# Two fused transformer blocks on one core: the first modulation and the stages' entries in another order, and identity products on TensorE at its waits

## The chip, the cores and the metric

One of the eight cores of a Trainium2 chip runs the whole program in one launch. The metric is the device time of one execution in microseconds. The engines are named as the profile names them: PE (TensorE matmul), PEld (its weight loads), DVE (VectorE), ACT (ScalarE), POOL (GpSimd), SP (SyncE, which issues nearly all DMAs).

## The reference

A block of two layers (feed-forward, mixer, feed-forward; the first mixer is differential attention over 512 image and 256 context tokens, the second a Fourier mixer), then a block with sparse and banded attention and a mixture of experts, all in float32 with 1024 channels. What the change touches:

```python
def rms_norm(x, g):
    y = x32 * lax.rsqrt(jnp.mean(x32 * x32, axis=-1, keepdims=True) + EPS)
    return (y * g.astype(jnp.float32)).astype(x.dtype)

def swiglu(h, w_gu, w_d):
    g, u = jnp.split(h @ w_gu, 2, axis=-1)
    return (jax.nn.silu(g) * u) @ w_d

def ada_params(cond, w_mod, b_mod):
    m = jax.nn.silu(cond) @ w_mod + b_mod          # 9 vectors of 1024 per layer: shifts, scales, gates

for i in range(DEPTH):
    x = x + 0.5 * mx[2] * swiglu(modulate(rms_norm(x, norm_g[i, 0]), mx[0], mx[1]), ...)
    ...   # mixer with mx[3..5], second feed-forward with mx[6..8]; the same for the context y in layer 0
```

## The kernel before

The program is a row of stages, each a `Block` in which every engine has its own hand-written list of instructions, ordered by semaphores. At a block's end every engine drains its queue and all meet, so the next stage starts when the last of them is through. Channels lie on the partitions (8 tiles of 128) and tokens on the free axis. A float32 product of full precision is written as three products of a high and a low part (`three`: wh·xh, wh·xl, wl·xh), with ACT making the high part of weights and inputs and DVE (or POOL) the low part.

`start` loads x (`xy`) and computes the modulation vectors that the first feed-forward needs: 17 tiles of 128 outputs, in five parts (`parts`, four of 512 columns and a last one of 128). Each part is a product of the condition with a slab `w[c]` in four column groups of PE (L443), copied by ACT (`line`, L488), turned to columns by `turn` (L435), and added to its bias by DVE. Meanwhile ACT squares x tile by tile (`square_tile`, L254) and DVE sums the squares (`add_square`, L259).

The entry of most stages is a norm: PE sums the squares over channels (`sum_squares`, L269 and L272), ACT takes the root (`token_roots`, L286), DVE inverts it (`invert_roots`, L291), PE spreads the roots over the partitions with products against the identity (`spread_roots`, L279), and then, tile by tile, DVE scales x (L859), ACT adds the shift and makes the high part (L789), DVE the low part (L865), and PE takes the tile (L711 to L713). The weights of the first two slabs were prefetched; ACT and POOL split them meanwhile (`early_high`, `early_low`).

`feed_forward` runs phases of gate/up and down products over slabs of a ring with two slots (`ring`, s = 0 and 1). Per slab SP loads (L656), ACT makes the high part (`split`, L755), DVE the low part (`split`, L805), PE multiplies (L675 to L677), and ACT and DVE finish the result (`item`). `split_ahead` gives ACT and DVE the order: the split of the next slab stands before the item of this one. In two of the four feed-forwards DVE also computes the later modulation vectors (`sum_mod_turn`, L368), whose weights SP loads (`load_mod_turn`, L354); `mod=0` in the first, over 768 tokens (image and context), `mod=1` in the second. `gains_of_mods` turns them to gains before the last down phase. The four are, in order: ffn1 of layer 0 (768 tokens), ffn2 of layer 0, ffn1 of layer 1 and ffn2 of layer 1 (512 tokens each).

`first_mixer` has an entry of its own: `w_high(i)` (L1104) makes the high parts of six heads' weights, four of them from the prefetched slabs and the last two (Y and Z) from a slab that SP loads in the stage, and `in_high` (L1138) the high part of the input; PE starts with the first three heads (L1013 to L1015) side by side.

## Time and profile before

| | |
|---|---|
| three executions | 3363.56, 3373.28 and 3377.71 us, median 3373.28 us |
| the profiled execution | 3363.18 us by the same clock; its span in the trace is 3360.3 us |
| PE, PEld, DVE, ACT, POOL busy | 91%, 67%, 41%, 25%, 7% of the span |
[...]

[...] A plain float32 product of the program is two records in the trace, one that is declared as fp32r is one. A matmul's duration has a tail that overlaps the next one: steady steps are shorter than the durations.

### The profile page before, as it was taken

What the parts mean: (1) busy time and instruction counts of PE and PEld (TensorE: products, weight loads), DVE (VectorE), ACT (ScalarE), POOL (GpSimd) and SP (SyncE); (2) the same over time, 40 slices, a digit from 0 to 9 for tenths busy, and PEclk for the clock granted to TensorE, in tenths of its full rate; (3) what the DMA queues carried; (4) which work ended last, traced back from release to release, by engine and by line L of the source; (5) the groups of instructions that cost most, each with busy time, mean ns of one, the idle gap of its engine ahead of it and who ended that gap; (6) DMA issues with size and microseconds to landing.
All of it is one profiled execution on the core that took longest, in us unless ns stands there. A gap on an engine that the chain in (4) does not pass through costs nothing. (4 is left out here: it accounts for less than half of the span.)

```text
span 3360.3 us, 36972 instructions
## 1 busy us (share of the span) xinstructions
PE 3073.8 (91%) x14470; PEld 2264.8 (67%) x14470; DVE 1375.7 (41%) x2137; ACT 847.1 (25%) x1334; POOL 241.7 (7%) x273
## 2 busy tenths in 40 slices
PE   6999999799888899999999899999999689869996
PEld 4888888677644687877888546888788454343334
DVE  3646454535565463644333213333421284121112
ACT  3211111232354332223222202222323252011111
POOL 1000000001000100001000001000100151012220
PEclk8999999899998899999999999999999799979997
DMA  4423323211000354632232202232222200338883
GB/s 185 159 93 120 118 98 128 79 62 51 13 0 26 140 224 156 238 138 88 94 106 77 80 25 88 88 100 91 86 98 81 91 2 28 139 141 348 351 347 127
DMA packets 78198, 395.15 MB, mean 118 GB/s; under 512 B 17536, under 2 KB 19968, under 8 KB 51712
## 3 DMA queue, kind: packets, MB, share of 16 engines
q1 hardware_dynamic: 66560, 385.12, 31.0%
q0 software_dynamic: 11520, 8.43, 0.8%
q8 instruction: 78, 1.28, 0.2%
q14 instruction: 40, 0.33, 0.0%
HBM read 443.82 MB, written 16.78 MB: 137 GB/s over the span
## 5 line engine op out<-in xcount | busy, mean ns | idle before, releaser
L675 PE MATMUL ps<-h_high_ffn,weights_high_ffn 128*128 128x512 f32 (+1 forms) x1696 | 624.7, 368 | 13.6 <-DVE weights_low_ffn L805 8.8
L676 PE MATMUL ps<-h_low_ffn,weights_high_ffn 128*128 128x512 f32 (+1 forms) x1696 | 623.6, 368 | 0.0
L677 PE MATMUL ps<-h_high_ffn,weights_low_ffn 128*128 128x512 f32 (+1 forms) x1696 | 623.0, 367 | 0.0
L675 PEld LDWEIGHTS ps<-h_high_ffn,weights_high_ffn 128*128 128x128 f32 x1696 | 320.1, 189 | 69.6 <-issue 14.2
L677 PEld LDWEIGHTS ps<-h_high_ffn,weights_low_ffn 128*128 128x128 f32 x1696 | 320.1, 189 | 53.0
L676 PEld LDWEIGHTS ps<-h_low_ffn,weights_high_ffn 128*128 128x128 f32 x1696 | 320.2, 189 | 52.5
L675 PE MATMUL ps<-hidden_high_ffn,weights_high_ffn 128*128 128x512 f32 (+1 forms) x880 | 328.5, 373 | 17.1 <-DVE weights_low_ffn L805 9.7
L755 ACT ACTIVATE weights_high_ffn<-weights 128x2048 fp32r<-128x2048 f32 (+4 forms) x160 | 243.9, 1524 | 364.8 <-PE ps L677 275.6
L676 PE MATMUL ps<-hidden_low_ffn,weights_high_ffn 128*128 128x512 f32 (+1 forms) x880 | 327.0, 372 | 0.0
L677 PE MATMUL ps<-hidden_high_ffn,weights_low_ffn 128*128 128x512 f32 (+1 forms) x880 | 326.9, 372 | 0.0
L805 DVE TENSOR_TENSOR weights_low_ffn<-weights,weights_high_ffn 128x2048 fp32r<-128x2048 f32 (+4 forms) x160 | 289.7, 1811 | 88.7 <-ACT weights_high_ffn L755 87.1
L814 DVE TENSOR_TENSOR tmp<-ps,tmp 128x512 f32<-128x512 f32 x110 | 68.1, 636 | 430.0 <-ACT tmp L765 430.0
L765 ACT ACTIVATE tmp<-ps 128x512 f32<-128x512 f32 x110 | 58.6, 554 | 645.0 <-PE ps L677 641.3
L675 PEld LDWEIGHTS ps<-hidden_high_ffn,weights_high_ffn 128*128 128x128 f32 x880 | 167.8, 191 | 48.6 <-issue 10.1
L676 PEld LDWEIGHTS ps<-hidden_low_ffn,weights_high_ffn 128*128 128x128 f32 x880 | 167.9, 191 | 28.1
L677 PEld LDWEIGHTS ps<-hidden_high_ffn,weights_low_ffn 128*128 128x128 f32 x880 | 167.5, 190 | 28.6
L829 DVE SCALAR_TENSOR_TENSOR xy<-ps,mods,xy 128x512 f32 (+1 forms) x112 | 72.6, 672 | 262.2 <-PE ps L677 261.8
L2623 PE MATMUL ps<-big,work 128*64 128x512 f32 x768 | 171.6, 598 | 5.1 <-issue 4.1
L368 DVE CUSTOM_DVE_ANT_0 scratch_ffn<-scratch_ffn 128x1024 f32<-128x1024 f32 x127 | 151.4, 1220 | 1.6 <-DMA scratch_ffn<-in_w_mod 1.6
L2623 PEld LDWEIGHTS ps<-big,work 128*64 128x64 f32 x768 | 65.8, 138 | 107.0 <-issue 107.0
L254 ACT ACTIVATE tmp<-xy 128x512 f32<-128x512 f32 (+3 forms) x64 | 43.7, 684 | 364.4 <-DVE xy L829 150.8
L315 POOL TENSOR_TENSOR weights_low_ffn<-weights,weights_high_ffn 128x512 fp32r<-128x512 f32 x32 | 40.8, 1288 | 1214.6 <-ACT weights_high_ffn L306 1214.6
(399 smaller groups left out, 4303.4 us busy)
## 6 DMA issues: line engine op xcount, KB each, us to landing
weights<-in_ffn_gu SPq DMA_DIRECT2D x88, 1024.0 KB, 5.0
big<-in_w_exp_gu SPq DMA_DIRECT2D x32, 2048.0 KB, 9.6
scratch_ffn<-in_w_mod SPq DMA_DIRECT2D x35, 1536.0 KB, 6.4
weights<-in_ffn_d SPq DMA_DIRECT2D x24, 768.0 KB, 4.3
weights<-in_w_in SPq DMA_DIRECT2D x16, 1024.0 KB, 4.8
weights<-in_ffn_d SPq DMA_DIRECT2D x24, 640.0 KB, 3.9
weights<-in_w_exp_dn SPq DMA_DIRECT2D x15, 1024.0 KB
hbuf<-in_w_exp_dn SPq DMA_DIRECT2D x12, 1024.0 KB
```

The costliest lines, as they stand in the source:

```text
L254: scalar.activation(last_square[:, 0:cols], x, ACT.Square).then_inc(nm["squared"].sem, 1)
L315: gpsimd.tensor_tensor(quarter(w_low[:, s, :], c), quarter(ring.buf[:, s, :], c), quarter(w_high[:, s, :], c).bitcast(F32), ALU.subtract). ...
L368: vector.tensor_tensor_reduce(mod_w[b][:, j, :] if last else mod_product, mod_w[b][:, j, :], cond_row[:, c, :], 1.0, 0.0, ALU.mult, ALU.ad ...
L675: pe.matmul(out, wh, xh, start=(k == 0), stop=False)
L676: pe.matmul(out, wh, xl, start=False, stop=False)
L677: mm = pe.matmul(out, wl, xh, start=False, stop=(k == n - 1))
L755: scalar.activation(w_high[:, s, 0:n], ring.buf[:, s, 0:n], ACT.Copy).then_inc(high_done[s].sem, 1)
L765: scalar.activation(tmp[:, s, a:a + n], gate_up(s, 0, c), ACT.Silu).then_inc(silu_g[s].sem, 1)
L805: vector.tensor_tensor(w_low[:, s, 0:n], ring.buf[:, s, 0:n], w_high[:, s, 0:n].bitcast(F32), ALU.subtract).then_inc(ring.used[s], 1)
L814: vector.tensor_tensor(tmp[:, s, a:a + n], gate_up(s, 1, c), tmp[:, s, a:a + n], ALU.mult)\
L829: vector.scalar_tensor_tensor(x, down(s, c), g, x, ALU.mult, ALU.add)\
L2623: mm = pe.matmul(ps[b * CAP:(b + 1) * CAP, 2 + n % 2, :], gT[:, k, b * CAP:(b + 1) * CAP], w[:, k, :], start=(k == 0), stop=(k == KD - 1))
```

## The change

Five edits. (1) `start`: the 128-wide part comes first, two parts are in flight on SP, the norm of the first feed-forward (sum of squares, roots, spread) is moved into `start` between the products, and the first feed-forward is called with `rooted=True` and leaves it out. (2) `feed_forward`: SP reloads slot 0 ahead of the modulation's loads, and slot 1 behind the first ones. (3) `split_ahead` has a `pause`: the gains (and, for `mod=0`, the last `sum_mod_turn`) are done by DVE after the second item of the last down phase. (4) `first_mixer`: ACT's `w_high(3)` to `w_high(5)` stand between the `in_high`. (5) `keep_busy(pe, n)`: n products of the identity with itself into an unused PSUM bank; three ahead of each spread (nine places), and nine at nine places: after the spread in three feed-forwards and both mixers, at the end of three feed-forwards, and at the end of the first mixer's output projection.

```diff
+    def sum_squares(pe, cols, ahead=0):
+        pe.wait_ge(nm["summed"].sem, nm["summed"].at + ahead)
...
+    def keep_busy(pe, n):
+        for _ in range(n):
+            pe.matmul(ps[:, 4, 0:P], ident[:], ident[:], start=True, stop=True)
+
     def spread_roots(pe, cols):
+        keep_busy(pe, 3)
         pe.wait_ge(nm["rooted"].sem, nm["rooted"].at + 2)
...
     def start(nxt):
-        parts = [4 * P] * (MOD_BEFORE[0] // 4) + [MOD_BEFORE[0] % 4 * P]
+        parts = [MOD_BEFORE[0] % 4 * P] + [4 * P] * (MOD_BEFORE[0] // 4)
...
                 for c, n in enumerate(parts):
-                    if c > 0:
-                        sync.wait_ge(tables.sem, 16 * c)
-                        sync.dma_start(w[c][:], io["w_mod_first"][c, :, :, 0:n]).then_inc(tables.sem, 16)
+                    if c >= 2:
+                        sync.wait_ge(mod_landed[c % 2].sem, 16 * (c // 2))
+                    sync.dma_start(w[c][:], io["w_mod_first"][c, :, :, 0:n]).then_inc(mod_landed[c % 2].sem, 16)
...
+                product(0)
+                product(1)
+                pe.wait_ge(tables.sem, 32)
+                turn(0)
+                turn(1)
+                pe.wait_ge(const_set.sem, 2)
+                sum_squares(pe, NT, KD)
+                product(2)
+                spread_roots(pe, NT)
+                turn(2)
+                product(3)
+                turn(3)
+                product(4)
+                turn(4)
...
                 for c in range(len(parts)):
+                    if c == 2:
+                        token_roots(scalar, NT)
                     scalar.wait_ge(sm["product"].sem, c + 1)
                     scalar.activation(line[c][:], ps[:, c, 0:parts[c]], ACT.Copy).then_inc(sm["line"].sem, 1)
-                scalar.activation(warm[:, 0:1], eps[:], ACT.Sqrt)
...
+            first = 0
+            if early and j == 0 or pause is not None and j == len(phases) - 1:
+                first = 1
+                if j > 0:
+                    split(ph, 0, 1)
                 item(ph, 0, 0)
                 split(ph, 1, 0)
                 item(ph, 0, 1)
+                if j > 0:
+                    pause()
...
+                    if j == 0:
+                        first = 1
+                        load_slab(ph, 0, 0)
+                        if mod is not None:
+                            sync.wait_ge(in_low.sem, j0 + KD * ns)
+                            sync.dma_start(cond_row, io["cond"][:, 0:conds, :]).then_inc(small_landed.sem, 16)
+                            sync.dma_start(bmod[:], io["b_mod"][mod]).then_inc(small_landed.sem, 16)
+                            sync.dma_start(normg[:], io["norm_g"][mod]).then_inc(small_landed.sem, 16)
+                            for b in range(2):
+                                sync.wait_ge(mod_used[b].sem, w0[b])
+                                load_mod_turn(sync, b, 0)
+                        load_slab(ph, 0, 1)
...
+                if not rooted:
+                    sum_squares(pe, cols)
+                    spread_roots(pe, cols)
+                    keep_busy(pe, 9)
...
+                if ns == 1:
+                    keep_busy(pe, 9)
...
+                def last_mods():
+                    if mod == 0:
+                        sum_mod_turn(vector, 1, mod_turns - 1)
...
+                    gains_of_mods(vector, mod, *(((1, 2), (8,)) if mod == 0 else ((0, 1, 2), (2, 8))))
...
                 w_high(0)
                 token_roots(scalar, NT)
-                for i in range(1, 6):
+                for i in range(1, 3):
                     w_high(i)
...
                 for k in range(KD):
                     in_high(k, 0)
+                    if k in (0, 2, 4):
+                        w_high(3 + k // 2)
...
+                pe.wait_ge(fm["wo_added"].sem, 6)
+                keep_busy(pe, 9)
```

How the instructions stand: first PE at the program's start, through `start` and into the first feed-forward. Before:

```order
1 L443 MATMUL ps<-first_mod,cond_columns 32x512 x16
2 L435 MATMUL ps<-condition_rows,first_mod_line 128x2 x4
3 L443 MATMUL ps<-first_mod,cond_columns 32x512 x8
4 L435 MATMUL ps<-condition_rows,first_mod_line 128x2 x4
5 L443 MATMUL ps<-first_mod,cond_columns 32x512 x8
6 L435 MATMUL ps<-condition_rows,first_mod_line 128x2 x4
7 L443 MATMUL ps<-first_mod,cond_columns 32x128 x8
8 L435 MATMUL ps<-condition_rows,first_mod_line 128x2 x5
9 L406 UNCONDITIONAL_BRANCH
11 L269 MATMUL ps<-ones,tmp 128x1 x6
12 L272 MATMUL ps<-ones,tmp 128x1 x6
13 L279 MATMUL ps<-ident,inverse 128x128 x6
```

And changed:

```order
1 L440 MATMUL ps<-first_mod,cond_columns 32x128 x8
2 L440 MATMUL ps<-first_mod,cond_columns 32x512 x8
3 L447 MATMUL ps<-condition_rows,first_mod_line 128x2 x5
4 L269 MATMUL ps<-ones,tmp 128x1 x6
5 L272 MATMUL ps<-ones,tmp 128x1 x6
6 L440 MATMUL ps<-first_mod,cond_columns 32x512 x8
7 L278 MATMUL ps<-ident 128x128 x3
8 L284 MATMUL ps<-ident,inverse 128x128 x6
9 L447 MATMUL ps<-condition_rows,first_mod_line 128x2 x4
10 L440 MATMUL ps<-first_mod,cond_columns 32x512 x8
12 L440 MATMUL ps<-first_mod,cond_columns 32x512 x8
13 L447 MATMUL ps<-condition_rows,first_mod_line 128x2 x4
```

The norm's three groups moved from behind the block's end to between the products of the third and fourth part.

Second, ACT at the entry of the first mixer (`head_w_high_R` to `_Z` are the six heads' weights, `first_h_high` the input). Before:

```order
180 L1104 ACTIVATE head_w_high_R<-weights 128x1024
181 L286 ACTIVATE inverse<-ps,eps 128x6
182 L1104 ACTIVATE head_w_high_A<-weights 128x1024
183 L1104 ACTIVATE head_w_high_B<-weights 128x1024
184 L1104 ACTIVATE head_w_high_X<-weights 128x1024
185 L1104 ACTIVATE head_w_high_Y<-weights 128x1024
186 L1104 ACTIVATE head_w_high_Z<-weights 128x1024
187 L1138 ACTIVATE first_h_high<-first_h,mods 128x512 x8
```

And changed:

```order
181 L1155 ACTIVATE head_w_high_A<-weights 128x1024
182 L1155 ACTIVATE head_w_high_B<-weights 128x1024
183 L1189 ACTIVATE first_h_high<-first_h,mods 128x512
184 L1155 ACTIVATE head_w_high_X<-weights 128x1024
185 L1189 ACTIVATE first_h_high<-first_h,mods 128x512 x2
186 L1155 ACTIVATE head_w_high_Y<-weights 128x1024
187 L1189 ACTIVATE first_h_high<-first_h,mods 128x512 x2
188 L1155 ACTIVATE head_w_high_Z<-weights 128x1024
```

The first tile of the input now stands ahead of three weight parts, two of which wait for a load.

Third, SP at the entry of the second feed-forward (ffn2 of layer 0). Before:

```order
128 L641 DMA scratch_ffn_0<-in_cond 128x1024
129 L642 DMA bmod<-in_b_mod 128x144
130 L643 DMA normg<-in_norm_g 128x48
131 L354 DMA scratch_ffn_0<-in_w_mod 128x3x1024 x2
135 L656 DMA weights<-in_ffn_gu 128x2048
```

And changed:

```order
126 L667 DMA weights<-in_ffn_gu 128x2048
127 L677 DMA scratch_ffn_0<-in_cond 128x1024
128 L678 DMA bmod<-in_b_mod 128x144
129 L679 DMA normg<-in_norm_g 128x48
130 L359 DMA scratch_ffn_0<-in_w_mod 128x3x1024 x2
131 L667 DMA weights<-in_ffn_gu 128x2048
132 L359 DMA scratch_ffn_0<-in_w_mod 128x3x1024 x2
```

The first gate/up slab moved ahead of the modulation's five loads.

## Rows read from the trace of the kernel before

**Rows 1.** The page: PE's busy time, and the granted clock in 40 slices.
```profile
PE 3073.8 (91%) x14470; PEld 2264.8 (67%) x14470; DVE 1375.7 (41%) x2137; ACT 847.1 (25%) x1334; POOL 241.7 (7%) x273
...
PEclk8999999899998899999999999999999799979997
```

**Rows 2.** Timeline from 24 to 62 us: start, duration, instruction, [idle before <-releaser].
```profile
24.53 3.64 PE L443 MATMUL ps<-first_mod,cond_columns 128*32 128x512 f32 x16 [3.43 <-DMA first_mod<-in_w_mod_first]
...
24.74 0.84 ACT L254 ACTIVATE tmp<-xy 128x768 f32<-128x768 f32 x1 [1.02 <-DVE tmp L259]
...
36.04 1.87 PE L435 MATMUL ps<-condition_rows,first_mod_line 128*128 128x2 f32 x8
36.18 0.60 ACT L488 ACTIVATE first_mod_line<-ps 128x512 f32<-128x512 f32 x1 [7.34 <-PE ps L443]
...
50.89 2.69 PE L269 MATMUL ps<-ones,tmp 128*128 128x1 f32 x12 [0.73 <-PEq L406]
...
56.34 1.14 ACT L306 ACTIVATE weights_high_ffn<-weights 128x512 fp32r<-128x512 f32 x2
56.73 2.93 PE L279 MATMUL ps<-ident,inverse 128*128 128x128 f32 x12 [0.58 <-DVE inverse L291]
...
61.34 0.76 PE L711 MATMUL ps<-h_high_ffn,weights_high_ffn 128*128 128x512 f32 x1 [1.69 <-DVE h_low_ffn L865]
```

**Rows 3.** Stretches A:B: length, busy us of each engine, granted clock, DMA share, GB/s.
```profile
20.00:22.00 2.00, 1.10 (x8) 0.00 (x0) 1.07 (x2) 0.84 (x1) 0.00 (x0) 1.00 1.02 434
24.00:26.00 2.00, 1.47 (x8) 0.40 (x12) 0.71 (x1) 1.26 (x2) 0.00 (x0) 1.00 0.53 106
```

**Rows 4.** Timeline at the first mixer's entry.
```profile
653.48 2.35 POOL L978 TENSOR_TENSOR head_w_low_B<-weights,head_w_high_B 128x1024 fp32r<-128x1024 f32 x1
...
658.18 1.06 ACT L1104 ACTIVATE head_w_high_Y<-weights 128x1024 fp32r<-128x1024 f32 x1 [5.21 <-DMA weights<-in_w_qk]
...
660.09 1.32 ACT L1138 ACTIVATE first_h_high<-first_h,mods 128x512 fp32r<-128x512 f32 x2
...
661.79 0.77 PE L1013 MATMUL ps<-first_h_high,head_w_high_R 128*128 128x512 f32 x1 [8.45 <-DVE first_h_low L1221]
```

**Rows 5.** Timeline at the third slab of the second feed-forward.
```profile
1152.54 1.23 DVE L368 CUSTOM_DVE_ANT_0 scratch_ffn<-scratch_ffn 128x1024 f32<-128x1024 f32 x1 [1.57 <-DMA scratch_ffn<-in_w_mod]
...
1158.81 1.91 ACT L755 ACTIVATE weights_high_ffn<-weights 128x2048 fp32r<-128x2048 f32 x1 [8.56 <-DMA weights<-in_ffn_gu]
...
1160.75 2.29 DVE L805 TENSOR_TENSOR weights_low_ffn<-weights,weights_high_ffn 128x2048 fp32r<-128x2048 f32 x1 [4.49 <-ACT weights_high_ffn L755]
```

**Rows 6.** The same place: PE's row, and the stretch after it.
```profile
1163.17 0.79 PE L675 MATMUL ps<-h_high_ffn,weights_high_ffn 128*128 128x512 f32 x1 [7.39 <-DVE weights_low_ffn L805]
...
1159.90:1166.70 6.80, 3.52 (x8) 2.81 (x9) 5.17 (x6) 1.95 (x4) 0.00 (x0) 0.50 0.71 290
```

**Rows 7.** PE and DVE ahead of the last down phases of the first two feed-forwards.
```profile
603.69 1.23 DVE L368 CUSTOM_DVE_ANT_0 ps<-scratch_ffn 128x1024 f32<-128x1024 f32 x1
...
609.40 0.19 DVE L382 SCALAR_TENSOR_TENSOR mod_gain<-mods,normg 128x16 f32<-128x16 f32 x2
...
610.62 0.79 PE L675 MATMUL ps<-hidden_high_ffn,weights_high_ffn 128*128 128x512 f32 x1 [4.29 <-DVE weights_low_ffn L805]
...
1462.63 0.50 PE L675 MATMUL ps<-hidden_high_ffn,weights_high_ffn 128*128 128x512 f32 x1 [2.29 <-DVE weights_low_ffn L805]
```

**Rows 8.** Timeline between the second and the third feed-forward.
```profile
1513.90 1.02 PE L269 MATMUL ps<-ones,tmp 128*128 128x1 f32 x8 [1.76 <-PEq L635]
...
1517.14 2.07 PE L279 MATMUL ps<-ident,inverse 128*128 128x128 f32 x8 [0.57 <-DVE inverse L291]
...
1521.77 0.77 PE L711 MATMUL ps<-h_high_ffn,weights_high_ffn 128*128 128x512 f32 x1 [2.55 <-DVE h_low_ffn L865]
```

**Rows 9.** Two stretches around a run of transposes (L2467).
```profile
2962.00:2965.40 3.40, 3.40 (x17) 3.40 (x18) 2.69 (x12) 1.02 (x1) 0.00 (x0) 0.50 0.00 0
2965.50:2972.00 6.50, 5.30 (x45) 4.75 (x43) 2.81 (x11) 4.45 (x6) 0.00 (x0) 1.00 0.93 340
```

More of the change, by code:

```diff
@@ L445, in _, with turn @@
                     mm.then_inc(sm["product"].sem, 1)
-                    if c > 0:
-                        turn(c - 1)
-                turn(len(parts) - 1)
+                def turn(c):
+                    pe.wait_ge(sm["line"].sem, c + 1)
+                    for i in range(parts[c] // P):
+                        mm = pe.matmul(ps[:, c, 2 * i:2 * i + 2], line[c][:, i * P:(i + 1) * P], chosen[:],
+                                       start=True, stop=True)
+                    mm.then_inc(sm["turned"].sem, 1)
+                product(0)
[12 more added lines that the diff above has]
+                turn(4)
             @block.vector
@@ L537, in norm, with split_ahead @@
             shifted.at += KD
-    def split_ahead(eng, phases, split, item, before=None, early=False):
+    def split_ahead(eng, phases, split, item, before=None, early=False, pause=None):
         for j, ph in enumerate(phases):
@@ L869, in _ @@
                 vector.wait_ge(in_low.sem, j0 + KD * ns)
-                split_ahead(vector, phases, split, item, before, True)
+                split_ahead(vector, phases, split, item, before, True, None if mod is None else last_mods)
                 for s in range(2):
                     vector.wait_ge(added[s].sem, r0[s] + len(cuts) * dturns * ns)
-        normed(ns)
+        if not rooted:
+            normed(ns)
         split_early()
```

127 lines of the change are left out of this document (61 added, 66 removed).

## Prediction

> **What bounds the kernel now.** I read the page first: PE is busy 91% of the span and the other engines at most 41%, so the time is PE's work plus PE's idle time, and an edit pays only where PE waits or runs at the low clock. The clock line shows that the stages run near full speed and the start and the ends of stages at 0.7 to 0.9 [rows 1]. I then read the timeline at PE's longest waits, and asked at each what ended it and what that thing had waited for.
>
> At the start PE takes the modulation's slabs as they land: it idles 3.43 us ahead of the second, and the queue moves 434 GB/s while a slab comes but 106 between two [rows 2, 3], since each load is issued after the one before has landed. Only behind the last slab do the norm's products start, at 50.89, and the first gate/up product comes at 61.34 [rows 2]. At the first mixer's entry PE idles 8.45 us until 661.79; ACT had stood 5.21 us at head Y's weights, whose load ended at 658.18, and only then made the input's high part at 660.09 [rows 4]. In the second feed-forward PE idles 7.39 us until 1163.17, because the third slab's high part starts only when its load lands, at 1158.81, behind the modulation's loads [rows 5, 6]. In both places DVE ends the wait by the record, but it is the load that is late. The other waits are of 2 to 5 us: ahead of last down phases [rows 7] and at the entries of stages [rows 8].
>
> **The change, part by part.** Times are those of the profiled execution, in us; minus is a gain.
>
> *Price of one identity product.* No row shows one; the nearest is the group of sums, plain float32 products of 128 by 128 weights, 12 records in 2.69 at the low clock [rows 2] and 8 in 1.02 at the high one, tails included [rows 8]. A record is a step of 0.22 at the low clock and, by halving, 0.11 at the high one (0.13 with tails). A product is two records: 0.44 or 0.22. Three cost 1.3 or 0.65, nine 4.0 or 2.0, and the 108 in the program 48 if all ran at the low clock and in nobody's shadow.
>
> *Start: −9.5.* With two loads in flight the loads no longer bind: at 434 GB/s [rows 3] they are through well before PE can use the last slab. The chain is PE's own. ACT's last square ends at 24.74 + 0.84 = 25.6 [rows 2]. ACT then copies the first two lines (0.3 and 0.6), to 26.5, and `turn(1)` takes 1.87 at the low clock [rows 2], to 28.3. The sums are two groups like the one of 2.69 [rows 2], overlapping a little, 5.3: 33.6. The third product, a group of 3.64 with its tail [rows 2], adds 3.4: 37.0. Three identities 1.3: 38.3. The spread, 2.93 at the low clock and 1.5 at the high one, ends at 41.2 or, if the clock has risen under this unbroken work, at 39.5. What follows is then at the high clock, half of the rows' durations: turn 0.9, product 1.7, ACT's copy 0.75 with its hand-over (0.60 in the row), turn 0.9, product 1.7, copy 0.75, turn 0.9, DVE's sums 0.6, block boundary 0.5: 8.7, so the block ends near 48.2. Now ACT must still make four quarters of the first slab's high part, of which two took 1.14 [rows 2], to 50.5, then the first tile's high part 0.7 and DVE's low part 0.7: the first gate/up product at 51.9 instead of 61.34. Bounds: all at the low clock 59.0 (−2.3); ACT's quarters partly hidden, 50.7 (−10.6).
>
> *First mixer's entry: −5.9.* The input's first tile now stands ahead of the weights X, Y, Z. What ends last is then POOL's low part of B, 653.48 + 2.35 = 655.8 [rows 4], with the first tile's high and low part at about 654.8. The spread is over at about 653.3; nine identities behind it end between 655.3 and 657.3. So PE starts at about 655.9 instead of 661.79. Tile 3 needs ACT to be past Y's load (658.18): its high part is ready at about 660, and PE's first three tiles, about 2 us each, cover it until 662. Bounds: identities at the low clock −4.4; with the first products at the full clock too −6.7.
>
> *SP's order in feed-forwards: −5.2.* The slab lands ahead of the modulation's data, about 3.7 MB that at the 290 GB/s of the row [rows 6] take over 10 us, and ACT's high part is out of the way. But DVE has its order: three modulation sums of 1.23 stand ahead of the low part, and they start when the modulation's data land, 1152.54, and end at 1156.3. The low part (2.29) then ends at 1158.6 instead of 1163.0 [rows 5]. PE ran dry at 1163.17 − 7.39 = 1155.8, so 2.9 of the 7.39 stay: −4.5. The stretch up to 1166.70 is at clock 0.50 [rows 6]; a shorter wait saves a part of it, −0.7 by my choice. Bounds: 0 (the sums come later as their loads were pushed back) and −6.2. The first feed-forward shows no such wait, and gets nothing.
>
> *Pause in the last down phase: +0.3.* In the first feed-forward DVE's sums and gains stand ahead of a split and PE waits 4.29 [rows 7]. They are not removed, only set behind the second item, ahead of the second slab's low part: from 603.69 to the gains at 609.40 they are about 5.4 of work without the memset, nothing hides them but the slab in progress, so I expect a wait of about 5.1 there: +0.8. In the second, about 1 us of gains leaves the way to the wait of 2.29 [rows 7]: −0.5. Bounds: −4.3 (the wait goes) and +5 (the wait stays and a second comes).
>
> *The other identities: −0.6.* Four block ends have nine. Between the second and the third feed-forward PE idles 1.76 ahead of the sums, at the high clock for the first group and at the low one for the spread (2.07) [rows 8]. Nine at the high clock (2.0) fit nearly into what PE waits: they end about 0.6 after the boundary of before. If the clock holds, the sums and the spread save 1.6, net −1; if it falls nevertheless, +0.6 and more, +1.2 in all. I take even chances for three of them (−0.25 in all) and −1.2 where mixer 2 is entered, as the low clock lasts longest there. Three ahead of a spread lie in the wait for the roots (0.57 [rows 8]) and overshoot it by 0.7 at the low clock: about +0.3 to +0.6 at each of the last entries, +1.45 together less what the clock gives. Nine behind a spread end inside the wait of 2.55 for the first tile [rows 8] at the high clock; at the low one they are 1.3 late, but the entry is then paced by DVE's tiles and catches up. Together −0.6; bounds −6 (clock kept everywhere) and +8 (paid at the low clock, nothing kept).
>
> [...] [Rows 9] show a run of products against the identity, back to back at 0.50 for 3.40, and the stretch behind it at 1.00. [...]
>
> Sum: −9.5 − 5.9 − 5.2 + 0.3 − 0.6 = −20.9. The profiled execution took 3363.2, so 3342.3 there. It is the fastest of the four executions seen; their mean is 3369.4, and 3369.4 − 20.9 = 3348.5. I predict 3349.
>
> **The rivals.**
> A: the identities don't hold or raise the clock. For it: they multiply mostly zeros, and no row shows such work alone. Against: rows of float32 products of the same shape run into the high clock. Then the start gains 6.0 (spread and the four parts behind at the low clock, less loads' time), the mixer 4.4, the slab 5.2, the pause loses 0.3 and the others 6.1: −9.2, on the mean 3360.
> B: the third slab's wait stays, as DVE's sums, not the slab, turn out to be last. For it: DVE ends the wait in the record. Against: its sums ended 4.49 before the low part began [rows 5]. −15.7, 3354.
> C: the start runs at the low clock to its end, as the hand-overs between PE and ACT break its work up. −2.3 instead of −9.5: −13.7, 3356.
> D, the other side: the identities are paid in series. An engine's list is in order, so if PE stands in them when its data are ready, at every place, all 48 are added to the gains of 20.6 from the other parts: +27, 3397. It turns to a loss from 20.6 uncovered, which is 47 of the 108 products at the low clock. Against: PE waits 0.6 to 4 us at nearly every place where they stand.
> E: the clock is held everywhere and the pause removes its wait: about −30, 3339.
>
> **How the numbers follow.** Chances: my forecast 0.56, A 0.19, B 0.09, C 0.08, D 0.03, E 0.05. A measurement of this kernel can tell about 0.5% (17 us) from no change, so faster means below 3356.4. The forecast's own range is 3341 to 3357, and 0.49 of its 0.56 lie below the bound; with 0.03 of A, 0.05 of B, 0.03 of C and E, faster is 0.65. Slower, above 3390, is D with 0.01 from the tails of the others, 0.04. The same is 0.31. The range from 3334 to 3364 takes in E's far end, A, B and C; beyond it lie D and the tails.
>
> **What would show it.** Start: the first L711-like product near 52 in the changed profile, the loads landed by 37; near 59, and C is right. Mixer: PE's first head product near 656, and ACT's stop at Y behind the first tile. Third slab: a wait of about 2.9 instead of 7.39, ended by DVE. Pause: the wait of 4.29 gone from its place and one of about 5 a slab later. Clock: the spread between the second and the third feed-forward near 1.1 instead of 2.07, and identities of 0.22 each; if they read 0.44 and the spread 2.07, A is right. The prediction is wrong if identities end after the data they cover for, or if a transfer moved forward slows the one that PE waits for next.

## The result and the profile after

| | before | changed |
|---|---|---|
| executions | 3361.46 to 3378.80 us, 6 runs, median 3369.15 | 3336.05 to 3347.73 us, 6 runs, median 3341.32 |
| ratio to before, 95% interval | | 0.9923, 0.9905 to 0.9940 |
| span of the profiled execution | 3360.3 us | 3336.7 us |
| granted clock, mean | 0.950 | 0.961 |

The change makes the kernel 0.8% faster, 26 us by the ratio; the spans of the two profiled executions differ by 23.6. The predicted time was 3349, in the range 3334 to 3364. A second measurement of the same kernel (e9 below) gave 0.9943 (0.9920 to 0.9965), 19 us, so the gain is best taken as 19 to 26 us, and the predicted 20.9 lies in it. The granted clock is the profile's share of full speed; the low clock is a reading of 0.50 and the high one of 1.00, as in [rows 9]. Of the page, the rows that answer to [rows 1]:

```profile
PE 3079.3 (92%) x14686; PEld 2278.1 (68%) x14686; DVE 1376.8 (41%) x2137; ACT 846.4 (25%) x1333; POOL 243.9 (7%) x273
...
PEclk9999999999898999999999999999999799979997
```

PE has 216 records more (108 products of two records) and its busy time has grown by only 5.5 us: the new products add 35.3, and work that now runs at the high clock saves the rest. The start's slice went from 8 to 9, but it is 8 in e9, the same kernel.

The timeline of PE and ACT in the new start (columns as in [rows 2]):

```profile
25.32 0.74 ACT L506 ACTIVATE first_mod_line<-ps 128x128 f32<-128x128 f32 x2
25.72 2.26 PE L447 MATMUL ps<-condition_rows,first_mod_line 128*128 128x2 f32 x10 [3.26 <-ACT first_mod_line L506]
...
30.41 2.70 PE L272 MATMUL ps<-ones,tmp 128*128 128x1 f32 x12
33.03 3.64 PE L440 MATMUL ps<-first_mod,cond_columns 128*32 128x512 f32 x16
...
36.60 1.60 PE L278 MATMUL ps<-ident 128*128 128x128 f32 x6
...
38.03 1.50 PE L284 MATMUL ps<-ident,inverse 128*128 128x128 f32 x12
39.37 0.95 PE L447 MATMUL ps<-condition_rows,first_mod_line 128*128 128x2 f32 x8
...
48.54 2.19 ACT L311 ACTIVATE weights_high_ffn<-weights 128x512 fp32r<-128x512 f32 x4 [2.08 <-PEq L411]
...
52.44 0.77 PE L751 MATMUL ps<-h_high_ffn,weights_high_ffn 128*128 128x512 f32 x1 [4.87 <-DVE h_low_ffn L914]
```

No row of the chain waits for a load any more. PE's work is unbroken from 25.72 to 42.2 (then it waits twice for 0.72, for ACT's copies), the products turn to their short durations during it (the third part's take 3.64, the fourth's 1.92, and the spread takes 1.50 instead of 2.93), and behind the block's end ACT's four quarters (2.19 in all) stand ahead of the first tile. The first gate/up product comes at 52.44 instead of 61.34: 8.9 gained, where 9.5 were predicted, step by step within 0.6. That the clock rises here is read from e9, the same kernel: its granted clock is 0.50 from 30 to 36 us and 0.99 from 36 to 38. In this trace the column says 1.00 from 24 to 42, for the long durations too.

At the first mixer's entry (POOL, ACT, DVE and PE; it answers to [rows 4]):

```profile
643.29 2.37 POOL L1028 TENSOR_TENSOR head_w_low_B<-weights,head_w_high_B 128x1024 fp32r<-128x1024 f32 x1
...
643.50 3.17 PE L278 MATMUL ps<-ident 128*128 128x128 f32 x18
643.67 0.72 ACT L1189 ACTIVATE first_h_high<-first_h,mods 128x512 fp32r<-128x512 f32 x1 [1.83 <-DVE first_h L1267]
...
644.50 1.71 DVE L1274 SCALAR_TENSOR_TENSOR first_h_low<-first_h,mods,first_h_high 128x512 fp32r<-128x512 f32 x1 [0.20 <-ACT first_h_high L1189]
...
646.43 0.48 PE L1064 MATMUL ps<-first_h_high,head_w_high_R 128*128 128x512 f32 x1
```

The wait of 8.45 us is gone and PE starts at clock 1.0 (granted 1.00 from 646.5 to 650, before 0.50 from 661.8 to 664.5; the product takes 0.48 instead of 0.77). It starts as its nine identity products end, but they are hardly what held it: DVE's low part of the first tile took 1.71 us and ended at 646.21, only 0.2 earlier. The same instruction took 0.75 in the kernel before. Here it ran beside POOL's low part of B, which ended at 645.66, and it ended 0.55 behind it. From the spread's start to this product it took 5.5 us instead of 11.4. That looks like the 5.9 of the prediction, but the spread itself now starts later behind the roots, because three identity products stand ahead of it: from the end of DVE's roots (640.18; before 650.36) it is 6.2 us instead of 11.4, a gain of 5.2. Another 1.3 follows in the first tile, which before ran at the low clock (PE is ahead of before by 15.4 at this product and by 16.7 at the start of the second tile).

PE's waits at the slabs whose order was changed, and DVE's first modulation sum ahead of the third slab, answering to [rows 5, 6, 7]:

```profile
610.51 0.79 PE L715 MATMUL ps<-hidden_high_ffn,weights_high_ffn 128*128 128x512 f32 x1 [5.31 <-DVE weights_low_ffn L850]
...
1136.13 1.23 DVE L373 CUSTOM_DVE_ANT_0 scratch_ffn<-scratch_ffn 128x1024 f32<-128x1024 f32 x1 [1.11 <-DMA scratch_ffn<-in_w_mod]
...
1142.19 0.49 PE L715 MATMUL ps<-h_high_ffn,weights_high_ffn 128*128 128x512 f32 x1 [2.80 <-DVE weights_low_ffn L850]
...
1438.55 0.50 PE L715 MATMUL ps<-hidden_high_ffn,weights_high_ffn 128*128 128x512 f32 x1 [1.61 <-DVE weights_low_ffn L850]
```

The third slab's wait is 2.80 (predicted 2.9) and in this execution the clock does not fall behind it (1.00 from 1142.2 to 1146, where it was 0.50 in [rows 6]). DVE still idles 1.11 us until the modulation's data land, and three sums stand ahead of the low part. The pause has moved the wait of 4.29 one slab on and made it 5.31 (predicted about 5.1). The last one fell from 2.29 to 1.61.

Between the second and the third feed-forward (PE; it answers to [rows 8]):

```profile
1486.28 2.17 PE L278 MATMUL ps<-ident 128*128 128x128 f32 x18
1488.75 1.02 PE L269 MATMUL ps<-ones,tmp 128*128 128x1 f32 x8 [0.30 <-PEq L660]
1489.63 1.03 PE L272 MATMUL ps<-ones,tmp 128*128 128x1 f32 x8
1490.53 0.92 PE L278 MATMUL ps<-ident 128*128 128x128 f32 x6
1491.28 1.11 PE L284 MATMUL ps<-ident,inverse 128*128 128x128 f32 x8
1492.23 2.17 PE L278 MATMUL ps<-ident 128*128 128x128 f32 x18
1495.09 0.47 PE L751 MATMUL ps<-h_high_ffn,weights_high_ffn 128*128 128x512 f32 x1 [0.69 <-DVE h_low_ffn L914]
```

The nine products fill PE's wait for the last squares and the others its waits for the roots and the first tile; sums and spread run at the high clock throughout (granted 1.00 from 1486 to 1499; spread 1.11 instead of 2.07). From the sums' start to the first tile it is 6.34 us instead of 7.87.

### The profile page after: what moved, and what is told of

It is laid out like the page before. It is cut to its first block and busy times, and to the rows that moved or that the text cites. A ratio compares the mean times of both kernels' runs of the same rounds, so it can differ in the third digit from the quotient of the medians.

```text
span 3336.7 us, 37345 instructions
## 1 busy us (share of the span) xinstructions
PE 3079.3 (92%) x14686; PEld 2278.1 (68%) x14686; DVE 1376.8 (41%) x2137; ACT 846.4 (25%) x1333; POOL 243.9 (7%) x273
## 5 line engine op out<-in xcount | busy, mean ns | idle before, releaser
L715 PE MATMUL ps<-hidden_high_ffn,weights_high_ffn 128*128 128x512 f32 (+1 forms) x880 | 327.9, 373 | 19.3 <-DVE weights_low_ffn L850 12.1
```

What stands on the lines that cost most here:

```text
L715: pe.matmul(out, wh, xh, start=(k == 0), stop=False)
```

## The experiments

Each kernel was measured beside the kernel before on the same chip; the ratio is to it. The scatter of one kernel's executions is 6 to 22 us, so small effects are read from the stages of the traces.

**e1: no identity products.** The calls of `keep_busy` are taken out of the changed kernel.

```diff
     def spread_roots(pe, cols):
-        keep_busy(pe, 3)
...
-                    keep_busy(pe, 9)
```

> The changed kernel without any identity product (all five reorderings stay). If the identities hold the clock and the entries are paced by DVE, little of that reaches the end: the spread between the second and third feed-forward goes back from 1.1 to about 2.07 us and the first tiles behind it to clock 0.50, the sums ahead of it start about 0.6 us earlier, and the time is 2 to 5 us above the changed kernel (about 3344). If the identities cost more than they give (rival), it is 2 to 5 us below it. If most of the gain is theirs (second rival), it loses over 10 us and lands near 3355.

Measured: median 3347.78, ratio 0.9939 (0.9921 to 0.9958). The same place as above, without the products:

```profile
1492.72 1.43 PE L269 MATMUL ps<-ones,tmp 128*128 128x1 f32 x8 [1.76 <-PEq L655]
1494.02 1.85 PE L272 MATMUL ps<-ones,tmp 128*128 128x1 f32 x8
1496.43 2.08 PE L279 MATMUL ps<-ident,inverse 128*128 128x128 f32 x8 [0.57 <-DVE inverse L291]
1501.05 0.76 PE L746 MATMUL ps<-h_high_ffn,weights_high_ffn 128*128 128x512 f32 x1 [2.55 <-DVE h_low_ffn L906]
```

The clock falls to half during the sums (0.67 from 1492.7 to 1494.1) and stays there into the first tile (0.50 from 1494.1 to 1505), as before: 8.33 us from the sums to the first tile instead of 6.34, with the sums 0.7 sooner behind PE's last product (a wait of 1.76 in place of 2.17 of products and 0.30 of wait), net 1.3 more. The mechanism is shown at this place. What it is worth in the whole kernel is not: 0.9939 stands between the two measurements of the changed kernel, 0.9923 and 0.9943. About four fifths of the gain or more are there without any identity product.

**e2: identity products alone** on the kernel before.

```diff
+    def keep_busy(pe, n):
+        for _ in range(n):
+            pe.matmul(ps[:, 4, 0:P], ident[:], ident[:], start=True, stop=True)
+
     def spread_roots(pe, cols):
+        keep_busy(pe, 3)
...
+                    keep_busy(pe, 9)
```

> The kernel before with the identity products alone, at their places. By my theory the waits of 8.45 us (first mixer) and 7.39 us (third slab) stay and the clock rows at the entries rise to 1.0 only where PE does not wait longer than the products last: 1 to 5 us faster than before, 0.15% at most. By the rival (the clock is the gain) 10 us or more faster. By the other rival (paid in series) slower by up to 10 us.

Measured: 12 runs, median 3364.20, ratio 0.9989 (0.9976 to 1.0001): 4 us, and the long waits stay (at the first mixer 5.69 behind the nine products, at the third slab 8.04). The products are neither the gain nor paid in series.

**e3: DVE's order at the two waits that were left.**

```diff
+            if pieces and j == len(phases) - 1:
+                todo = list(pieces)
+                for t in range(turns - 1):
+                    for b in range(2):
+                        split(ph, t + b, 1 - b)
+                        item(ph, t, b)
+                        if todo:
+                            todo.pop(0)()
+                first = turns - 1
...
                 split(ph, 1, 0)
+                if j == 0 and behind is not None:
+                    behind()
                 item(ph, 0, 1)
```

`pieces` are the four reductions of the last modulation sum and the gains, for `mod=0`; `behind` is the first modulation sum of `mod=1`, which now stands behind the third slab's low part.

> The changed kernel with DVE in another order at two places: in the first feed-forward's last down phase the last sum of the modulation is cut into its four reductions and the gains, one behind each of five items; in the second feed-forward the third slab's low part stands ahead of the first modulation sums. If DVE's order is what PE waits for, the wait of 5.31 us at 610.5 shrinks below 1 us and that of 2.80 us at 1142.2 below 0.8 us, and with the clock behind them the time falls by 7 to 11 us, to about 3332. If the load of the slab or of the modulation weights is behind the second wait (rival), only about 5 us are gained. If the pieces break the steady rhythm of the down phase, five waits of about 1 us come in place of the one and nothing is gained there.

Measured: median 3335.70, ratio 0.9909 (0.9887 to 0.9931). The timeline of DVE and PE at the second feed-forward's third slab and in the first's last down phase:

```profile
1134.16 2.29 DVE L861 TENSOR_TENSOR weights_low_ffn<-weights,weights_high_ffn 128x2048 fp32r<-128x2048 f32 x1 [1.11 <-ACT weights_high_ffn L810]
1136.37 1.22 DVE L373 CUSTOM_DVE_ANT_0 scratch_ffn<-scratch_ffn 128x1024 f32<-128x1024 f32 x1
...
602.12 0.49 PE L726 MATMUL ps<-hidden_high_ffn,weights_high_ffn 128*128 128x512 f32 x1 [0.92 <-DVE weights_low_ffn L861]
...
606.89 0.50 PE L726 MATMUL ps<-hidden_high_ffn,weights_high_ffn 128*128 128x512 f32 x1 [0.32 <-DVE weights_low_ffn L861]
```

The low part starts at 1134.16, straight after ACT's high part, with the sums behind it, and PE has no wait there at all. In the down phase waits of 0.92, 0.32, 0.48 and 0.31 stand in place of the one of 5.31: DVE idled about 1.5 us of each slab before, but 1.1 of them in the middle of its item, waiting for ACT's square, so that with a reduction of 1.2 its round takes 4.8 us where a slab took 4.2. The stage is 3.2 us shorter than in the changed kernel (580.8 from the first gate/up product to the next norm's sums, against 584.0), and the one of the second feed-forward 3.5 (370.2 against 373.7); in e8, which has the same order, they are 582.5 and 372.6, so the gain of a stage is 1 to 3.5 us against that trace. By the ratios this kernel and e8 are the fastest of the study, 5 to 11 us faster than the two measurements of the changed one, but the intervals overlap. The order of DVE, not the slab's load, was what the two waits were made of.

**e4: dense operands.**

```diff
-            pe.matmul(ps[:, 4, 0:P], ident[:], ident[:], start=True, stop=True)
+            pe.matmul(ps[:, 4, 0:P], dense[:], dense[:], start=True, stop=True)
```

> The changed kernel with the identity products replaced by as many products of a full 128x128 piece of x with itself (results unused, one more small load at the start). If the operands' values do not matter for the clock, entries and time are as with the identity: within 3 us of the changed kernel, the spread between the second and third feed-forward at 1.1 us. If products of mostly zeros count less for the clock (rival A of the prediction in another form), the clock at the first mixer's entry, 0.57 between 640.0 and 646.5 us, rises to 0.8 or more and the time falls by 3 us or more.

Measured: median 3349.17, ratio 0.9939 (0.9916 to 0.9963).

```profile
1492.24 2.17 PE L279 MATMUL ps<-dense 128*128 128x128 f32 x18
1494.70 1.02 PE L270 MATMUL ps<-ones,tmp 128*128 128x1 f32 x8 [0.30 <-PEq L662]
...
1497.23 1.11 PE L285 MATMUL ps<-ident,inverse 128*128 128x128 f32 x8
```

Every duration is that of the identity (2.17, 1.02, 1.11), and the first mixer's entry takes 9.9 us in both, at a granted clock of 0.66 in both. At these places a product of mostly zeros holds the clock as well as a dense one; with e1, where the same spread without them takes 2.08, rival A falls.

**e5 and e6: the reorderings alone**, on the kernel before and without identity products: e5 has only the new start, e6 only the two orders below (the diff is e6's).

```diff
-                for i in range(1, 6):
+                for i in range(1, 3):
                     w_high(i)
...
                     in_high(k, 0)
+                    if k in (0, 2, 4):
+                        w_high(3 + k // 2)
...
+                        load_slab(ph, 0, 0)
                         if mod is not None:
                             sync.wait_ge(in_low.sem, j0 + KD * ns)
```

> The kernel before with the new start alone (and the norm of the first feed-forward in it), no identity product, the other edits undone. The first gate/up product should come near 50.6 us, as in the run without identities, instead of 61.34, and the 10 to 11 us should persist to the first mixer's entry and to the end: about 0.30% faster than before. Rival: most is given back where DVE and POOL pace the first tiles, so that at the first down phase less than 7 us is left.

> The kernel before with only the first mixer's ACT order and SP's order in the feed-forwards. By the terms of the prediction: wait of 8.45 us at the first mixer down to about 2.6 (-5.9; without identities the first products there run at clock 0.50, so nothing more), wait of 7.39 at the third slab down to 2.8 to 2.9 (-4.5 and 0.7 to 1.6 of clock): together 11 to 12 us, 0.33% faster than before. Rival: the terms need the identities' clock and only 8 us are seen.

Measured: e5 median 3359.07, ratio 0.9973 (0.9960 to 0.9985), 9 us; e6 median 3353.23, ratio 0.9954 (0.9940 to 0.9968), 15 us. PE's rows at the first gate/up product of e5, and at the first mixer and the third slab of e6:

```profile
51.04 0.76 PE L731 MATMUL ps<-h_high_ffn,weights_high_ffn 128*128 128x512 f32 x1 [4.87 <-DVE h_low_ffn L888]
```

```profile
655.41 0.77 PE L1028 MATMUL ps<-first_h_high,head_w_high_R 128*128 128x512 f32 x1 [3.18 <-DVE first_h_low L1238]
...
1158.34 0.49 PE L690 MATMUL ps<-h_high_ffn,weights_high_ffn 128*128 128x512 f32 x1 [2.82 <-DVE weights_low_ffn L820]
```

The start gains 10.3 us alone and still had 10 at 900 us. At the second feed-forward's sums only 7.3 were left, and at the end of the two profiled executions 3.3: stages that no edit of e5 touches took longer in this execution, the second half of the first mixer above all (3 us), and the one of the kernel before was some 6 us faster than its median. The mixer's wait fell by 5.3 to 3.18, and from the roots to its first product the gain is the 5.3 of that wait as well; counted from the sums it is 5.7. The third slab's wait fell by 4.6. Neither needs an identity product. The parts add up within the noise: 0.27 + 0.46 + 0.11% for e5, e6 and e2, which is 0.84% without the pause, each known to some 0.13%, against 0.57 to 0.77% for the whole.

**e7: twice as many identity products.**

```diff
-        for _ in range(n):
+        for _ in range(2 * n):
```

> The changed kernel with six identity products ahead of each spread and eighteen where there were nine. If the products of the changed kernel just fill PE's waits, the added ones are paid at most places: three more at 0.22 to 0.44 at nine spreads (6 to 12 us less what is still waited for, 0.57 at one place) and nine more at nine places at 0.22 (2.0 each, less the waits of 0.7 left behind them): together 15 to 25 us slower than the changed kernel, some 3363, with the clock at 1.0 at every entry. Rival: where the entry is paced by DVE's tiles, PE catches up and less than 8 us are seen.

Measured: 12 runs, median 3370.53, ratio 1.0003 (0.9989 to 1.0017).

```profile
1497.34 4.18 PE L278 MATMUL ps<-ident 128*128 128x128 f32 x36
...
1503.60 1.58 PE L278 MATMUL ps<-ident 128*128 128x128 f32 x12
...
1505.91 4.18 PE L278 MATMUL ps<-ident 128*128 128x128 f32 x36
1509.85 0.48 PE L751 MATMUL ps<-h_high_ffn,weights_high_ffn 128*128 128x512 f32 x1
```

The 108 more cost the whole gain: 20 to 27 us against the changed kernel, 0.19 to 0.25 us each, which is about a product's full price at the high clock (108 x 0.22 = 24). So on the whole the products of the changed kernel already fill the waits, and rival D's mechanism is real beyond them. At single places they fall short of the wait or overshoot it: at this norm PE still waited 0.69 behind them, ahead of the last feed-forward not at all.

**e8: placed anew**, on e3.

```diff
-        keep_busy(pe, 3)
+        keep_busy(pe, ahead)
...
-                    spread_roots(pe, cols)
+                    spread_roots(pe, cols, 0 if name == "ffn2" and i == 1 else 3)
...
-                spread_roots(pe, NT)
-                keep_busy(pe, 9)
+                spread_roots(pe, NT, 2)
+                keep_busy(pe, 5)
...
-                if ns == 1:
-                    keep_busy(pe, 9)
+                keep_busy(pe, 9, 4 if ns == 1 else 5)
```

> The kernel of e3 with the identity products placed anew: none ahead of the spread in the start and at the four entries where the sums run at the low clock anyway (second feed-forward of layer 1, the spread in the start, the router's norm, the last norm), five instead of nine at the first mixer's entry, and nine also at the end of the first feed-forward. By the reading of the run without identities the start gets 0.6 to 1.8 us back, the other places 0.7 each, and the sums at the first mixer's entry run at clock 1.0 (-1.3): 3 to 5 us below e3, about 3331. Rival: the clock falls at the places where products were taken away and the time is that of e3 or above.

Measured: median 3338.16, ratio 0.9909 (0.9890 to 0.9928), that of e3. At the first mixer's entry:

```profile
631.38 2.17 PE L278 MATMUL ps<-ident 128*128 128x128 f32 x18
633.91 1.47 PE L269 MATMUL ps<-ones,tmp 128*128 128x1 f32 x12 [0.35 <-PEq L671]
635.24 1.48 PE L272 MATMUL ps<-ones,tmp 128*128 128x1 f32 x12
```

The sums there do run at clock 1.0 (granted 1.00 from 633.9 to 636.6), and from them to the first product it is 9.5 us (11.1 in e3, 9.9 in the changed kernel), but the start did not become faster (first product at 51.4, in e3 at 51.2), and the expected 3 to 5 us were not seen. Part of what the sums gained is lost behind them: DVE's low part of the first tile started sooner and took 2.67 instead of 1.71, again until 0.55 behind the end of POOL's low part of B, and PE waited 1.76 for it. From the roots to the first product it is 6.2, as in every trace with the new order but e7's.

**e9: the changed kernel again.**

> The changed kernel once more, on the chip of these runs, to be set against e5, e6 and e8 and to see how much one stage varies between two profiled executions of the same program: the attention stage between its first product near 2625 us and the router's sums took 284.9, 290.9 and 297.4 us in three programs that are alike there. I expect a median of 3341 to 3345 and a stage between 284 and 298 us, set by the share of it at the low clock.

Measured: median 3346.44, ratio 0.9943 (0.9920 to 0.9965). At the first mixer's entry the nine products end earlier here, and PE does wait for DVE's low part:

```profile
644.23 2.36 POOL L1028 TENSOR_TENSOR head_w_low_B<-weights,head_w_high_B 128x1024 fp32r<-128x1024 f32 x1
...
645.42 1.72 DVE L1274 SCALAR_TENSOR_TENSOR first_h_low<-first_h,mods,first_h_high 128x512 fp32r<-128x512 f32 x1 [0.20 <-ACT first_h_high L1189]
...
647.29 0.47 PE L1064 MATMUL ps<-first_h_high,head_w_high_R 128*128 128x512 f32 x1 [1.06 <-DVE first_h_low L1274]
```

The attention stage took 284.1 us here. Stretches of that stage in the changed kernel and, below, in e2 (columns as in [rows 3]):

```profile
2624.80:2909.70 284.90, 251.91 (x1316) 140.25 (x1316) 141.64 (x488) 90.21 (x337) 74.97 (x120) 0.94 0.13 49
```

```profile
2645.70:2943.00 297.30, 266.09 (x1316) 148.56 (x1316) 142.07 (x488) 89.97 (x337) 74.97 (x120) 0.88 0.12 47
```

The same 1316 products, and 12.4 us between them, at a mean clock of 0.94 and 0.88. No edit touches this stage. The stretch from the first mixer's attention to its output projection is another: 188.3 in the first profile of the changed kernel, 192.1 in this one.

**e10: the pause undone.**

```diff
-                if j > 0:
-                    pause()
...
                     if j == len(phases) - 1:
                         clear_squares(vector, cols)
+                        if mod is not None:
...
+                            gains_of_mods(vector, mod, *(((1, 2), (8,)) if mod == 0 else ((0, 1, 2), (2, 8))))
```

> The changed kernel with the pause undone: the gains and the last sum stand ahead of the last down phase again. The wait of about 4.3 us returns ahead of the first slab of that phase, the one of 5.31 behind the second goes, and the stretch from the first to the second norm's sums (584.0 and 586.1 us in the two profiles of the changed kernel) is 1.0 to 1.5 shorter, about 583. In the second feed-forward the wait of 1.61 goes back to 2.3. Net 0.5 to 1 us faster, not to be told from the changed kernel by its time.

Measured: median 3343.44, ratio 0.9924 (0.9909 to 0.9938). The wait ahead of the down phase is back:

```profile
603.31 0.50 PE L715 MATMUL ps<-hidden_high_ffn,weights_high_ffn 128*128 128x512 f32 x1 [2.70 <-DVE weights_low_ffn L850]
```

It is 2.70, not 4.3 (2.72 and 2.70 in e2 and e6, and why it differs from the 4.29 of before is not shown), and the one in the second feed-forward is 2.29 again. The stage is 583.0. The time shows no effect of the pause, but the stages do, against it: from the first gate/up product to the next norm's sums the five traces without the pause took 581.9 to 583.4 us, the seven with it and without e3's order 583.8 to 587.8.

**e11 and e12: which of the places does it.** e11 has the products at the four block ends alone, e12 all but these.

```diff
     def spread_roots(pe, cols):
-        keep_busy(pe, 3)
...
                     spread_roots(pe, cols)
-                    keep_busy(pe, 9)
```

```diff
-                if ns == 1:
-                    keep_busy(pe, 9)
```

> The changed kernel with the identity products at the four block ends alone (nine each), none ahead of a spread and none behind one. Without any the stages from the second norm to the spread of the fifth lost 8 us and the start gained 1.8. If the ends do the work, the sums and spreads behind them stay at clock 1.0 (spread of 1.1 us), the start keeps its 1.8, and the time is at or below the changed kernel's (3340 to 3343). If the products behind the spread are needed to keep the clock until the first tile, the first products of the feed-forwards run at 0.50 again and each entry loses about 1 us: 3345.

> The changed kernel without the nine products at the four block ends, with those ahead of and behind the spreads. By the reading that the ends keep the clock, the sums behind a block's end fall to the low clock (2.7 to 3.2 us for both groups instead of 1.9), the three ahead of the spread take 1.6 instead of 0.9 and delay it, and the products behind it overlap the first tile: 1 to 2 us lost at each of the four, some 3347. By the rival, that the ones behind the spread do the work, it is as fast as the changed kernel.

Measured: e11 median 3350.55, ratio 0.9930 (0.9907 to 0.9953); e12 median 3355.23, ratio 0.9945 (0.9925 to 0.9964). PE in e11, then in e12, at the same norm:

```profile
1506.08 1.02 PE L269 MATMUL ps<-ones,tmp 128*128 128x1 f32 x8 [0.30 <-PEq L659]
...
1508.57 1.16 PE L283 MATMUL ps<-ident,inverse 128*128 128x128 f32 x8 [0.57 <-DVE inverse L295]
1512.40 0.77 PE L750 MATMUL ps<-h_high_ffn,weights_high_ffn 128*128 128x512 f32 x1 [2.68 <-DVE h_low_ffn L912]
```

```profile
1499.72 1.59 PE L278 MATMUL ps<-ident 128*128 128x128 f32 x6
1501.10 1.91 PE L284 MATMUL ps<-ident,inverse 128*128 128x128 f32 x8
```

With the ends alone it is 6.32 us from the sums to the first tile, as with all (6.34), although the first tile itself runs at the low clock (granted 0.50 from 1512.4 to 1515, its first product 0.77); with the others alone it is 7.62. What the products behind the spread keep fast is then paced by DVE's tiles. This does not hold at the first mixer: in the traces with the new order and products behind the spread PE gained 1.1 to 1.4 us on before over the first tiles, and in e1, e6 and e11, which have the order without these products, it lost 0.7 to 1.4. The times of e11 and e12 agree with the ends doing more, but are within each other's intervals.

## Why the prediction was right, and where it was off

PE's first product of a stage, in us from the start; the last two columns are how much earlier than before it came in the two profiled executions of the changed kernel:

| | before | changed | earlier by | in e9 |
|---|---|---|---|---|
| first feed-forward | 61.34 | 52.44 | 8.9 | 9.8 |
| first mixer | 661.79 | 646.43 | 15.4 | 14.5 |
| second feed-forward | 1131.40 | 1115.08 | 16.3 | 11.5 |
| third feed-forward | 1521.77 | 1495.09 | 26.7 | 20.0 |
| last feed-forward | 2053.31 | 2028.45 | 24.9 | 19.9 |
| behind the router's norm | 2948.34 | 2922.41 | 25.9 | 21.4 |
| span | 3360.3 | 3336.7 | 23.6 | 19.6 |

The gains are made where the prediction put them. That the forecast's sum of −20.9 lies between the two is in part luck, as the terms show.

**Start, −9.5.** Measured −8.9 (52.44), −9.8 in e9 (51.6), −10.3 alone. The chain was the predicted one: PE's own work from ACT's last square on, then ACT's quarters. The choice between the two bounds, that the clock rises under unbroken work, was right (the spread took 1.50 in both traces); rival C did not come. The three identity products ahead of the spread, priced at 1.3, took 1.4, cover no wait there and are a cost.

**First mixer, −5.9.** The mechanism was right, the size 0.7 too large: −5.2 from the roots to the first product in the changed kernel, −5.3 in e6 and e9. The prediction let PE start when POOL's low part of B ends, and had the first tile's low part ready 1.0 us before that. In fact DVE's low part ended 0.55 us behind POOL's, in each of ten traces with the new order, whether it took 1.71 or 2.67 us, and PE started 0.15 to 0.22 later. The nine identity products gave no earlier start: it is 6.2 us from the roots with them and without. What they gave is the clock of the first tiles, 1.3, which the prediction had only in its bound. A further 2.1 came from the sums at this entry, which took 3.2 us instead of 5.3. No term had them, and no edit explains them: no product stands ahead of them, and in the traces without one there they took 2.9 to 5.3.

**Third slab, −5.2.** The cause was the predicted one in the main: the slab's load no longer counts, and what is left is DVE's sums, which e3 shows by moving them. The sums still start when the modulation's data land. The wait was 2.80 in the changed kernel, 3.25 in e9 and 2.82 in e6; from the last products ahead of it to the 24th behind it PE gained 6.2, 4.2 and 4.6. So the 0.7 for the clock came as 1.6 in the first execution and as nothing in the other two. Rival B fell.

**Pause, +0.3.** The waits were +1.0 and −0.7, the predicted +0.8 and −0.5, but the low clock behind the longer wait (0.50 from 610.5 to 614; 0.54 before, 1.00 in e10) was left out of the sum. Behind its first gate/up product the first feed-forward took 0.8 us more than before in the changed kernel and 2.8 more in e9, and 1.1 and 3.1 more than in e10. In the second feed-forward the shorter wait gives 0.7 back. So the pause was a small cost, somewhat larger than predicted, and no time of a whole kernel can tell it.

**Other identity products, −0.6.** This was the weakest term, and its working does not close: −0.25, −1.2 and +1.45 add up to nothing, and the −0.6 rests on a gain by the clock that got no number of its own. In the eight traces with nine products at the block ends the clock held until the spread (1.1 to 1.2 us instead of 2.07) at the second feed-forward in all eight, at the third in six, at the Fourier mixer in three (not in the changed kernel's first trace, where the spread took 1.92 and the entry 11.8 us instead of 11.3) and at the second block's first norm in none. Where it held, 0.9 to 1.5 was seen from the sums to the first tile, less the 0.7 that the sums now start later behind PE's last product. Where no nine stand ahead (the last feed-forward of layer 1) the entry took 9.8 us instead of 8.7, and at the router 12.7 instead of 12.1: three products ahead of a spread cost 0.5 to 1.1 there, where +0.3 to +0.6 a place was foreseen. Of the −1.2 where the Fourier mixer is entered the changed kernel's first trace shows nothing, and e9 −1.0 (10.3 instead of 11.3), less the same 0.7. e2 gives 4 us for all products together, with zero at the edge of its interval; so between 0 and 8. Rival D was rightly held small for 108 products and would have been right for 216.

The forecast of 3349 lies 8 us above the first measurement and 3 above the second. The two profiled executions of the changed kernel are 4 us apart, and one stretch of the first mixer that no edit touches differs by as much (3.8 us, under e9); no cause is claimed for it.

## What to carry to other kernels

Ask of a long wait which transfer or which item in an engine's list is late, and move that item past the one that waits: such moves (e5, e6) gave nearly all of this gain, and two more (e3) another 5 to 11 us, though this is not clear of the noise. Filler work can hold TensorE's clock, here not at every place: in the changed kernel's first trace the spread took 1.11 us instead of 2.07 between the second and the third feed-forward, but 1.81 at the second block's first norm. Its best place was the end of a block, where PE would idle until the other engines are through (from the sums to the first tile 6.32 us with the block ends alone, 7.62 with the other places alone). It must be sized to the wait: 108 products more cost 0.19 to 0.25 us each. At the entry that DVE's tiles paced, a faster clock of the first tile gave nothing (6.34 us against 6.32). Two executions of one kernel differ by several us in stages that nobody touched, so check a term on a second trace before you call its size measured.

## What the runs showed of the hardware

Identity and dense data made no difference for the granted clock between the second and the third feed-forward: it read 1.00 with both, and the durations were the same, 2.17 us for nine products and 1.11 for the spread behind them.

The 108 identity products of plain float32 are 216 records in the trace. A record's duration has a tail that overlaps the next one: in the kernel before, 128x512 products of 0.63 us followed each other every 0.43 at the low clock (from 1164.19), and products of 0.39 every 0.23 at the high one (from 700.88).

One instruction of DVE took longer where one of POOL ran beside it: the low part of the first tile at the first mixer took 0.75 us in the four traces in which POOL's low part of B had ended before it began, and 1.71 to 2.67 in the ten in which the two overlapped, ending 0.55 behind POOL's each time.

The moment at which the clock rises under the same unbroken work differs between executions: the spread in the start took 1.50 us in the changed kernel, and in kernels without identity products there 1.60 (e1, e5) and 2.57 (e11). The granted clock was 1.00 from 36 to 38 us in e1 and 0.63 from 37 to 40 in e11. The first gate/up product moved with it, from 50.6 in e1 to 52.6 in e11, whose start is the same program; of these 2.0 us 0.7 were there before the unbroken work began (25.59 and 26.30).

A stage that no edit touches took between 283 and 297 us in the traces of this study, at mean clocks from 0.95 down to 0.88. The stretch from the first mixer's attention to its output projection took between 187.6 and 194.4. By these ranges, 14 and 7 us, the two alone can make a large part of the 6 to 22 us between the executions of a kernel; this is an estimate, as each range is over several kernels.
